# Layer 0's prompt and sample attention in one block of 32 slots

## What is computed

```python
# prompt: 8 forgetting heads (64 wide) and 4 differential heads (2 x 64), causal
pa = softmax(where(causal, qa @ ka.T * scale + (cq - ck), -inf));  oa = pa @ va
pb = softmax(where(causal, qb @ kb.T * scale, -inf))               # two per head
ob = rms_norm((pb[:, :, 0] - lam * pb[:, :, 1]) @ vb, subln0) * (1 - LAMBDA_INIT)
# each of the 8 samples: the same, over cache_k[page_table[b]] (8 pages of 128 x 1024)
# followed by its own 8 new keys and values
yp = yp + mp @ w_out0;  ys = ys + ms @ w_out0                       # then a gated FFN
```

## Time and profile before

| | us |
|---|---|
| median of 3 runs | 1888.01 |
| the runs | 1884.02 to 1888.47 |
| the profiled execution | 1890.89 |
| its span in the trace | 1888.7 |
| projection's last matmul to output product's first | 221.8 to 519.0 |
| of that, prompt attention's matmuls | 227.8 to 320.8 |
| sample attention's matmuls | 322.7 to 515.9 |

### The profile page before, as it was taken

One profiled execution on the slowest core, in us unless ns is written; L12 is line 12 of the kernel. 1 busy time (PEld: TensorE's weight loads), 2 busy tenths in 40 slices (PEclk: granted clock), 3 DMA queues, 4 the chain that ended last, 5 costly groups with the idle time before them and its releaser, 6 DMA issues. The chain is left out here.

```text
span 1888.7 us, 30754 instructions
## 1 busy us (share of the span) xinstructions
PE 1706.5 (90%) x11686; PEld 1417.9 (75%) x11694; DVE 861.4 (46%) x1680; ACT 607.1 (32%) x1267; POOL 124.8 (7%) x166
## 2 busy tenths in 40 slices
PE   5998897889798999999998787687888999999998
PEld 4787565655488998899987575354557999889987
DVE  4446536455434332323325978985545232223323
ACT  3325465233223222122213344554333232112220
POOL 1222003100000000000000012110000000000000
PEclk9999898899998999999998899788889999999999
DMA  5232210899632322333221112102742322233221
GB/s 183 68 117 79 99 64 14 323 391 388 244 100 61 89 80 72 96 97 103 84 79 55 49 45 53 40 1 58 211 133 66 89 68 82 84 90 86 70 84 67
DMA packets 177022, 201.31 MB, mean 107 GB/s; under 512 B 21651, under 2 KB 131539, under 8 KB 176915
## 3 DMA queue, kind: packets, MB, share of 16 engines
q1 hardware_dynamic: 167634, 189.39, 31.5%
q10 hardware_dynamic: 9200, 10.24, 1.7%
q0 software_dynamic: 80, 0.26, 0.1%
HBM read 190.77 MB, written 9.08 MB: 106 GB/s over the span
## 5 line engine op out<-in xcount | busy, mean ns | idle before, releaser
L209 PE MATMUL ps<-feat_lo,w_hi 128*128 128x288 f32 x1408 | 416.6, 296 | 7.4 <-PEq L2154 3.8
L211 PE MATMUL ps<-feat_hi,w_hi 128*128 128x288 f32 x1408 | 416.6, 296 | 0.0
L210 PE MATMUL ps<-feat_hi,w_lo 128*128 128x288 f32 x1408 | 416.3, 296 | 0.0
L191 DVE TENSOR_TENSOR w_lo<-w_raw,w_hi 128x2048 fp32r<-128x2048 f32 x96 | 220.1, 2293 | 343.7 <-ACT w_hi L185 343.4
L185 ACT ACTIVATE w_hi<-w_raw 128x2048 fp32r<-128x2048 f32 x96 | 183.7, 1914 | 347.7 <-PE ps L217 343.3
L209 PEld LDWEIGHTS ps<-feat_lo,w_hi 128*128 128x128 f32 x1408 | 265.8, 189 | 8.6 <-issue 4.4
L210 PEld LDWEIGHTS ps<-feat_hi,w_lo 128*128 128x128 f32 x1408 | 265.8, 189 | 0.0
L211 PEld LDWEIGHTS ps<-feat_hi,w_hi 128*128 128x128 f32 x1408 | 265.7, 189 | 0.0
L2254 DVE TENSOR_TENSOR f_prod<-f_silu,ps 128x576 f32<-128x576 f32 x44 | 33.2, 754 | 361.4 <-ACT f_silu L2233 361.4
L209 PE MATMUL ps<-w_lo,feat_hi 128*128 128x512 f32 (+1 forms) x448 | 181.9, 406 | 12.5 <-DVE feat_lo L2106 5.5
L210 PE MATMUL ps<-w_hi,feat_lo 128*128 128x512 f32 (+1 forms) x448 | 178.0, 397 | 0.0
(11 more groups left out here) (331 smaller groups left out, 2363.9 us busy)
## 6 DMA issues: line engine op xcount, KB each, us to landing
s_vslot<-in_cache_l_v_dram SPq DMA_DIRECT2D x64, 512.0 KB, 8.5
s_kslot<-in_cache_l_k_dram SPq DMA_DIRECT2D x56, 512.0 KB, 10.3
w_raw<-in_w_gate_dram SPq DMA_DIRECT2D x44, 512.0 KB, 4.0
w_raw<-in_w_up_dram SPq DMA_DIRECT2D x44, 512.0 KB, 5.2
w_raw<-in_w_in_dram SPq DMA_DIRECT2D x18, 1024.0 KB, 5.2
w_raw<-in_w_down_dram SPq DMA_DIRECT2D x16, 1024.0 KB, 5.0
s_kslot<-in_cache_l_k_dram SPq DMA_DIRECT2D x56, 128.0 KB, 2.6
w_raw<-in_w_down_dram SPq DMA_DIRECT2D x8, 768.0 KB, 4.4
```

The lines of the kernel that those rows point to most:

```text
L191: dve.tensor_tensor(self.K.w_lo[:, n % 2, :], self.K.w_raw[:, n % 2, :], self.K.w_hi[:, n % 2, :].bitcast(F32), ALU.subtract).then_inc(sel ...
L209: pe.matmul(out, lhs[0], rhs[1], start=start, stop=False)
L210: pe.matmul(out, lhs[1], rhs[0], start=False, stop=False)
L211: return pe.matmul(out, lhs[0], rhs[0], start=False, stop=stop)
```

## The change

`FirstAttention` takes the place of both attention stages of layer 0. It is one block without loops, of 32 slots. Slot x = 4b + k holds prompt unit x, the turning of two key pages (2x and 2x + 1, so sample b's eight pages in four slots), the scoring of sample b's pages one or two at a time behind it, and two value pages of sample b - 1. Mixed pairs come first, and the query tiles in the order 2, 1, 3, 0. The prompt has one set of score banks. All transposes (keys, probabilities, outputs) go through two banks, ring a, which ACT empties, and ring b, which DVE empties. Filling the sample's queries and rounding its bias rows is POOL's. Pages stand in twelve places that cover `w_raw`, `w_hi` and `w_lo` whole; so `Weights.held` keeps the first two tiles of the output product out of the projection, and they are loaded at the new block's end: the first is also split there, the second in the output product.

Its core (`...` marks what is left out; the three loops over x are TensorE's, ACT's and DVE's, in this order):

```diff
     def load_up_to(self, sp, last):
+        if self.held is not None:
+            last = min(last, self.held - 1)
@@
-        if n + 2 < len(self.tiles):
+        if n + 2 < (len(self.tiles) if self.held is None else self.held):
             eng.wait_ge(*self.used[n])
             half(eng, n + 2)
@@
+class FirstAttention:
+    KEY_PLACES, VALUE_PLACES, TURNED_PLACES = 5, 4, 3
+    QT_ORDER = (2, 1, 3, 0)
+    PAIR_ORDER = (4, 5, 6, 7, 0, 1, 2, 3)
+    SQUARES, SUM, SPREAD = 18, 22, 24
...
+        def ring(x):
+            if filled[x]:
+                pe.wait_ge(emptied[x], filled[x])
+            filled[x] += 1
+            return self.RING[x]
+        def scores(u):
+            p, qt = self.units[u]
+            w, diag = self.width(u), slice(qt * P, (qt + 1) * P)
+            if u:
+                pe.wait_ge(S["exped"], 2 * u)
...
+        def score_into(dst, keys_at):
+            for x in range(2):
+                for i in range(4):
+                    c = 2 * i + x
+                    ins = pe.matmul(dst[self.rows4[i], :], self.qz[:, c, self.rows4[i]], keys_at(c), start=False,
+                                    stop=True, skip_group_check=True)
+            return ins
...
+        for x in range(self.SLOTS + 1):
+            b, k = divmod(x, 4)
+            if k == 1 and b >= 2:
+                turn_o(b - 2)
+            if x < self.SLOTS:
+                scores(x)
+                turn_keys(2 * x)
+            before = b - 2 if k == 0 else b - 1
+            first = (6, 0, 2, 4)[k]
+            if before >= 0:
+                weigh_page(before, first)
+            if x:
+                turn(x - 1)
+            if x < self.SLOTS and k:
+                score_page(b, 2 * k - 2)
+            if x < self.SLOTS:
+                turn_keys(2 * x + 1)
+            if before >= 0:
+                weigh_page(before, first + 1)
+                if k == 0:
+                    weigh_news(before)
+            if x < self.SLOTS and k:
+                score_page(b, 2 * k - 1)
+            if x < self.SLOTS and k == 3:
+                score_news(b)
...
+            if x:
+                weigh(x - 1)
+            if x < self.SLOTS and k == 3:
+                score_page(b, 6)
+                score_page(b, 7)
+            if k == 0 and b:
+                turn_probs(b - 1)
+        turn_o(LAST - 1)
+        for j in range(N_PAGES):
+            weigh_page(LAST, j)
+        weigh_news(LAST)
+        turn_o(LAST)
...
+        for x in range(self.SLOTS + 1):
+            if x >= 2:
+                finish(x - 2)
+            if x < self.SLOTS:
+                keys_out(2 * x)
+            if k == 0 and b:
+                sample_exps(b - 1)
+            if x:
+                head_out(x - 1)
+            if x < self.SLOTS:
+                exps(x)
+                keys_out(2 * x + 1)
...
+        finish(self.SLOTS - 1)
+        act.wait_ge(S["page_scored"], N_PAGES * DEC_BATCH)
+        K.weights.hi(act, self.next_tile)
...
+        for x in range(self.SLOTS + 1):
+            if k == 0 and b:
+                shift(b - 1)
+            if x:
+                blend(x - 1)
+            if k == 1 and b >= 2:
+                o_finish(b - 2)
+            if x >= 2:
+                finish(x - 2)
+            if x < self.SLOTS:
+                top(x)
+                keys_out(2 * x)
+            if x:
+                head_out(x - 1)
+            if k == 3 and b < DEC_BATCH:
+                first_top(b)
+            if x < self.SLOTS:
+                keys_out(2 * x + 1)
...
+            if x < self.SLOTS:
+                sums(x)
+            if k == 0 and b:
+                sample_probs_out(b - 1)
...
+    def sync(self, sp):
+        for sem, count in K.unstored:
+            sp.wait_ge(sem, count)
...
+        load_bias(0)
+        for x in range(-3, self.SLOTS + 3):
+            for half in range(2):
+                g = 2 * x + half + self.KEY_PLACES
+                h = 2 * x + half - 6
...
+                if 0 <= g < G:
+                    load_key(g)
...
+                if h == G - 2:
+                    load_new(DEC_BATCH - 1)
+                    K.weights.load_up_to(sp, self.next_tile)
+                if self.VALUE_PLACES <= h < G:
+                    load_value(h)
+        sp.wait_ge(S["value_used"], G - 2)
+        K.weights.load_up_to(sp, self.next_tile + 1)
```

More of the change, by code:

```diff
@@ L152, in __init__ @@
         self.split_hi, self.split_lo = sem("weights_split_hi"), sem("weights_split_lo")
-        self.used, self.late = {}, None
+        self.used, self.late, self.held = {}, None, None
     def leave(self, n):
@@ L2762, in two_layers @@
                                  for name, shape in (("c_rows", [P, SEQ]), ("c_sel", [P, FOX, P])))
+            W.held = out0[0][0][0]
             with ExitStack() as beside:
                 project(nc, K, parts, "p0", side=ForgetGates(nc, K, beside, f_rows))
-            def half_rows(i):
-                return slice(i * HEAD_DIM, (i + 1) * HEAD_DIM)
-            def values0(p, i, j):
-                return vp[:, j, (2 * p + i) * HEAD_DIM:(2 * p + i + 1) * HEAD_DIM] if p < FOX // 2 else \
-                    vp[:, j, 512 + (p - FOX // 2) * P:512 + (p - FOX // 2 + 1) * P]
@@ L2772, in two_layers @@
-            retired, K.phase_sems = K.phase_sems, []
-            early = EarlyKeys(nc, K, "s0", K.cache_l0_k, None)
-            prompt_attention(
-                nc, K, "a0", q_at=lambda p, i, qt: qp[half_rows(i), p, qt * P:(qt + 1) * P],
-                k_at=lambda p, i: kp[half_rows(i), p, :], v_at=values0, gates=True, mask=None,
-                mixed=lambda p: p >= FOX // 2, early_keys=early, retired=retired)
+            retired, K.phase_sems = K.phase_sems, []
+            first_out, W.held = W.held, None
@@ L2778, in two_layers @@
+            with ExitStack() as mem:
+                FirstAttention(nc, K, mem, qp, kp, vp, qs, ks, vs[0:DEC_SEQ, :], retired, first_out).block()
             for h in retired:
                 nc.release_semaphore(h)
-        def fill_q0(dve, qz, b, ok):
-            flat = qz[:, :, :].rearrange("p c n -> p (c n)")
-            for half in range(2):
-                rows = slice(half * HEAD_DIM, (half + 1) * HEAD_DIM)
-                for c in range(KC):
-                    col = c * P + 16 * c + 8 * half
-                    ins = dve.tensor_copy(flat[rows, col:col + DEC_SEQ], qs[rows, c, ds(b * DEC_SEQ, DEC_SEQ)])
-            ins.then_inc(ok, 1)
@@ L2791, in out0_fn @@
-        def out0_fn(dve, OT, b):
-            now = ds(b * DEC_SEQ + SEQ, DEC_SEQ)
-            for x in range(2):
-                o = OT[:, x, :].rearrange("p (i x a q) -> p i x a q", i=4, x=2, a=2)[:, :, x]
-                for half in range(2):
-                    rows = slice(half * HEAD_DIM, (half + 1) * HEAD_DIM)
-                    dve.tensor_copy(K.att[rows, x:4:2, now], o[rows, 0:2, half, :])
-                ins = dve.tensor_reduce(K.att[:, 4 + x:8:2, now], o[:, 2:4].rearrange("p i a q -> p i q a"), AX, ALU.add)
-            return ins
@@ L2848, in two_layers, with half_rows @@
             project(nc, K, parts[1:], "p1", side=top)
+            def half_rows(i):
+                return slice(i * HEAD_DIM, (i + 1) * HEAD_DIM)
             early = EarlyKeys(nc, K, "s1", K.cache_l1_k.rearrange("n k g d -> n k (g d)"), 2 * BANK)
@@ L2949, in build @@
         K.feat_lo = sb("feat_lo", [P, KC, TOK], F32R)
+        K.free0 = nc.alloc_sbuf_tensor_at("free0", [P, 2 * KC * P + KEYS], F32, offset=feat_hi_at)
+        bias_at = feat_hi_at + (2 * KC * P + KEYS) * 4
+        K.bias_rows = nc.alloc_sbuf_tensor_at("bias_rows", [32 + 2 * FOX, KEYS], F32R, offset=bias_at)
+        K.bias_raw = nc.alloc_sbuf_tensor_at("bias_raw", [SAMP + 2 * FOX, KEYS], F32, offset=bias_at)
         K.att = nc.alloc_sbuf_tensor_at("att", [P, KC, TOK], F32, offset=feat_lo_at)
```

765 lines of the change are left out of this document (460 added, 305 removed).

## The result

| | before | after |
|---|---|---|
| median (13 runs each) | 1888.0 us | 1893.5 us |
| runs from, to | 1884.0, 1890.7 | 1889.7, 1897.1 |
| profiled execution, its span | 1890.9, 1888.7 | 1892.0, 1890.2 |
| first prompt matmul to first matmul of the output product | 291.2 us | 294.3 us |
| DMA issues in the stretch, landing | 512 KB, 5.3 us | 512 KB, 4.5 us (keys), 5.1 us (values) |

The ratio is 1.0032 (95%: 1.0024 to 1.0040): the changed kernel is slower by 0.3%, where 0.3% less was forecast. The forecast was 1881.9.

A forecast was written before the change was run, and what follows sets the result against it. TensorE bounds the loop, transfers right behind. 231.9 (start) + 2.5 (slow clock) + 261.0 (cycles and norm) + 17.5 (end) = 512.9 against 519.0, 6.1 us less: 1888.0 - 6.1 = 1881.9 us; 8-in-10 range 1864 to 1904.

The forecast's parts named there:

- Start: Block's start: matmuls from 225.8, first key transposes at 231.9 us, then 2.5 us lost to TensorE at 1.2 GHz.
- Work and waits in the cycles: Cycles of four slots: 31.6 us mixed (25.0 work, 2.6 switches, 4.0 waits), 34.8 plain (29.7, 2.6, 2.5).
- five waits of a mixed cycle: TensorE's waits: 1.6 before second key page, 0.9 ring b, 0.5 turned output, 0.45 `o_finish`, 0.5 late blends; 4.0 us.
- those for `o_finish` and for late blends: Mixed cycle: next key page in k = 1 waits 0.45 us for `o_finish`; late blends add 0.5.
- the one for DVE's wide maximum: Plain cycle: the second head's turning waits for DVE's wide maximum, within 2.5 us of waits.
- Switches: Changes between the array's full width, quarters and halves: 0.13 us each, 0.65 a slot, 2.6 a cycle.
- the rival's 0.27: Slower rival, switches at the upper bound of 0.27 us each: 22 us more, 1904; chance 0.22.
- The norm: Prompt norm in the block: 48 small matmuls at 0.117 us add 5.6 us.
- The end: From last score to output product: 17.5 us, including 1.7 for value pages 6 and 7; held weights loaded beside this.
- From profile to median: Profiled execution before stood 2.9 us above its median, so 1884.8 profiled became a forecast of 1881.9.
- the rival's 18 us: Slower rival, clock falling in slots: mixed slots at 0.84, 16% of time at 1.2 GHz, 1900 us; chance 0.08.
- Pages late: Rival: slots wait for transfers or instructions; 0.3 us a slot makes 1892, 0.6 makes 1901; chance 0.06.

The follow-up runs named there:

- The experiment: Changed kernel with SP's first key page issued ahead of its wait for the projection's stores and the bias rows: ratio 1.0015 to the kernel before.
- The split: Changed kernel with the norm's sums taken one head at a time, eight one-column matmuls in each of slots 19 to 22: ratio 1.0021 to the kernel before.
- the second profile: Changed kernel run again without any edit, in a second series: ratio 1.0041 to the kernel before, stretch 296.5 us.
- the same exchange of order: Changed kernel, ACT emptying ring a before the sample's exponentials in slots k = 0: 1.0042; with the prompt's exponentials also behind the second key page: 1.0000, against 1.0041.

## Why the prediction was wrong

The steps that failed are two: the end, where the late transfers were weighed against TensorE's work and not against the queue (17.5 us for 23.9), and the norm, whose matmuls were priced as if the clock stayed up (5.6 for 9.6). The sum was made for the output product's first matmul: 512.9 forecast, 521.2 in the first profile. Counted from the prompt's first matmul, forecast for 225.8, it is a stretch of 287.1 us, and 294.3 were measured.

- **Start**: right. The first key transposes were to come 6.1 us behind the first matmul and came 6.15 and 6.19 behind it. In the first profile both stand 1.1 to 1.2 us later than forecast (226.9, 233.1), and 0.7 of that is there already at the projection's last matmul, which the change doesn't touch; in the second they stand at 225.6 and 231.8. The experiment takes 1.0 us off a term that was rightly sized.
- **Work and waits in the cycles**: right in the sum, less so in the terms. 30.9 for 31.6, 34.4 and 34.7 for 34.8. Three of the five waits of a mixed cycle came, 2.6 us in place of 4.0; those for `o_finish` and for late blends did not, and work and switches hold 0.7 more instead. (The terms of a sample's work add up to 18.25, where 18.1 was used.) In a plain cycle the same three waits stand, not the one for DVE's wide maximum, so that 2.5 was met by 2.6 by luck.
- **Switches**: right. 0.12 each was measured in place of 0.13, and 0.11 for leaving the quarters. The Trainium skill (TensorEngine Tiling (Array Packing), Key Properties) has the drain at a change of mode; the 0.12 agrees that it costs time, and the rival's 0.27 is not its price at these shapes. What the longer start in the earlier trace rows holds besides wasn't tried.
- **The norm**, 5.6 forecast and 9.6 measured: the step that failed is costing its matmuls at the pace of a kernel at full clock. The cycle with the row of 32 lost 6.7 us for 3.7: 0.8 of it within the row (4.5 for 3.7), the rest in the slots behind it, which ran at 1.2 GHz. The split gave back 2.3, as its own first row costs 0.5 more than its work. The four spreads took 2.8 for 1.9; one wait of 0.4 for DVE is in that, the rest was not followed up.
- **The end**, 17.5 forecast and 23.9 measured: the step that failed is "at 2 to 5.3 us each in parallel, while weighing pages 1 to 5 covers 2.3", with the held tile "loaded beside this". I weighed value pages 6 and 7 against TensorE's work only, and not against the queue: the tile of 1 MB went out in front of them (502.8 and 505.8), pages 2 to 5 had been asked for only after 498, and the queue was full (1.03). TensorE waited 6.4 us for pages, as much as the excess, and asking earlier took it away (16.6). In this place the clock also fell to 0.50.
- **From profile to median**: the forecast took 2.9 us off because the execution before stood that far above its median. The stretch explains 7.2 of the 11.6 us between forecast and median (1892.0 against 1884.8 in profiled executions); the other 4.4 are this 2.9 and the 1.5 by which the profiled execution after ran below its median. From the product's first matmul to the end the execution before took 1369.7 us, among the 1368.3 to 1371.9 of nearly all others, so the 2.9 doesn't lie there. Whether it was right to take it off stays open, as the kernel before has only one profile.
- **The rivals**: none of the named ones came in. The granted clock was 1.00 in the third and fourth mixed cycle; it fell behind the norm's row, now and then in the first mixed cycle, and at the end. (A mean of 0.84 is 32% of the time at 1.2 GHz, not 16%; the rival's 18 us are what that costs, about. And the trace before shows falls outside the mixed pairs too, 0.79 from 321 to 346.) "Pages late" was the nearest, but I had put it into each slot; the slots' transfers never waited, and it was the block's end that did.

Of the 7.2 us the start has 0.1, the cycles 0.7 and the end 6.4. In the 0.7 the norm's 4.0 and -3.3 from the cycles cancel, of which about 2.5 are the luck of the first mixed cycle. So luck hid most of the norm's miss in this profile; the second profile's stretch, 296.5, is 9.4 above the forecast.

## What to carry to other kernels

When two stages are merged so that each covers the other's waits, sum up the bytes that are asked for after the last covering work has begun, at the rate that the queue has shown; here reordering them gave nothing in the ratio and asking earlier 6.6 us. Follow a wait that is removed to the end of its slot: the same exchange of order gave nothing or 7.7 us, by one more step, and of ring b's 8.9 us of waits half came back one instruction later. Price a small thing by cycles that no change of the clock touches (30.88 and 30.90 us here), not by whole runs. And compare a second profile of the same kernel before a difference of 2 us is read from one.

## What the hardware showed that I had not expected

- Behind a row of 32 one-column matmul records the granted clock fell to 1.2 GHz while TensorE was never idle (0.52 and 0.51 in the windows over its end and behind it; 0.68 in another execution); with eight at a time it stayed at 1.00.
- Four quarter-width matmuls run side by side: 0.46 us for the four of 256 columns, and 0.56 with the switch for two of them alone. A switch between quarters and full width cost 0.12 us.
- In one kernel the granted clock between 262 and 270 us was 1.00 in one execution and 0.57 and 0.58 in another, of the same program. What decides it wasn't found.
